# A mixer's seven block products: two weight sums by accumulating DMA, quadrant-wise weights, another product order

## The reference

```
def mixer_block(u, cos, sin, w_in, conv_w, q_norm_g, k_norm_g, w_conv_out, w_attn_out, w_o):
    proj = u @ w_in
    cb, cc, cx, q, k, v, gc, ga = split_columns(proj)
    z = depthwise_conv_centred(cc * cx, conv_w)
    y_conv = (cb * z) @ w_conv_out
    ...
    y_attn = bidirectional_gqa(q, k, v) @ w_attn_out
    merged = jax.nn.sigmoid(gc) * y_conv + jax.nn.sigmoid(ga) * y_attn
    return merged @ w_o
```

## Time and profile before

| | before |
|---|---|
| time, median of 3 runs | 1936.64 us (1935.13 to 1938.69) |
| profiled execution: span from first to last instruction | 1937.6 us |
| PE busy | 1576.1 us (81% of the span) |
| DVE busy | 683.6 us (35%) |
| ACT / POOL busy | 303.4 us (16%) / 13.0 us (1%) |
| bytes by DMA | 554.48 MB, mean 286 GB/s |
| granted TensorE clock, mean | 0.913 |

### The profile page before, as it was taken

The page is one execution under the profiler, slowest core; times in us unless marked ns, Lnnn a source line. Parts: engine busy times, 40 slices in busy tenths (PEclk is TensorE's granted clock), DMA queues, the critical chain, the costliest instruction groups (busy, mean ns, idle before and its releaser), DMA issues.

```text
span 1937.6 us, 22198 instructions
## 1 busy us (share of the span) xinstructions
PE 1576.1 (81%) x9674; PEld 958.1 (49%) x9674; DVE 683.6 (35%) x1421; ACT 303.4 (16%) x806; POOL 13.0 (1%) x39
## 2 busy tenths in 40 slices
PE   8999999999999999856655756556666557799999
PEld 6675566755599995322212222212222122357886
DVE  2673455734486873311111111101111111244533
ACT  0243313433112102000000000000000000213220
POOL 0000000000000000000000000000000000000000
PEclk9999999999999999988778887788787788899999
DMA  9752277413334466999999999999999999954300
GB/s 378 264 138 71 87 272 239 124 51 135 129 137 174 146 236 270 388 431 431 430 431 432 431 430 430 429 427 426 424 426 431 432 431 431 374 205 165 126 14 22
DMA packets 87787, 554.48 MB, mean 286 GB/s; under 512 B 4512, under 2 KB 11424, under 8 KB 74112
## 3 DMA queue, kind: packets, MB, share of 16 engines
q1 hardware_dynamic: 86544, 548.81, 70.4%
q0 software_dynamic: 1136, 4.10, 0.6%
HBM read 551.85 MB, written 1.05 MB: 285 GB/s over the span
## 4 chain that ended last, share of the span: by engine, by line
PE 59%; DMA 35%; DVE 4%; ACT 1%; issue 1%; SPq 0%; POOL 0%; DVEq 0%; ACTq 0%; POOLq 0%
PE bank L677 26%; DMA ring<-in_w 22%; DMA arena<-in_w 12%; PE bank L1154 8%; PE bank L704 6%; PE bank L686 6%; PE bank L1182 3%; PE bank L665 3%; PE bank L1467 1%; PE bank L875 1%; PE bank L809 1%; PE bank L789 1%; DMA prm<-in_pk 1%; DVE arena L2122 0%; DVE arena L2402 0%
## 5 line engine op out<-in xcount | busy, mean ns | idle before, releaser
L1154 PE MATMUL bank<-ring,arena 128*32 128x512 f32 x1216 | 289.1, 732 | 152.0 <-DMA arena<-in_w 100.7
L677 PE MATMUL bank<-arena,ring 128*128 128x128 f32 (+1 forms) x2528 | 393.7, 315 | 0.5 <-DVE arena L3071 0.5
L677 PEld LDWEIGHTS bank<-arena,ring 128*128 128x128 f32 x2528 | 357.2, 191 | 28.2 <-issue 4.5
L1154 PE MATMUL bank<-arena 128*32 128x512 f32 x832 | 234.1, 734 | 100.2 <-DMA ring<-in_w 100.2
L1154 PEld LDWEIGHTS bank<-ring,arena 128*32 128x32 f32 x1216 | 72.1, 131 | 274.6 <-issue 274.6
L677 PE MATMUL bank<-ring,arena 128*128 128x512 f32 (+3 forms) x520 | 205.2, 544 | 1.7 <-ACT tmp L1523 0.8
L1154 PEld LDWEIGHTS bank<-arena 128*32 128x32 f32 x832 | 56.7, 131 | 187.3 <-issue 187.1
L1182 PE MATMUL bank<-ring,arena 128*32 128x512 f32 x576 | 119.3, 660 | 25.2 <-DMA arena<-in_w 13.9
L677 PEld LDWEIGHTS bank<-ring,arena 128*128 128x128 f32 x520 | 96.1, 190 | 84.0 <-issue 72.3
L704 PE MATMUL bank<-ring,arena 128*128 128x512 f32 (+1 forms) x320 | 129.1, 561 | 4.6 <-DVE arena L2003 2.2
L686 PE MATMUL bank<-arena,ring 128*64 128x256 f32 x1024 | 112.7, 380 | 0.0
(11 more groups left out here) (395 smaller groups left out, 1482.7 us busy)
## 6 DMA issues: line engine op xcount, KB each, us to landing
ring<-in_w SPq DMA_DIRECT2D x53, 4096.0 KB, 31.7
arena<-in_w SPq DMA_DIRECT2D x35, 4096.0 KB, 36.9
ring<-in_w_in SPq DMA_DIRECT2D x40, 2048.0 KB, 8.2
ring<-in_w_mod SPq DMA_DIRECT2D x6, 2048.0 KB, 11.9
ring<-in_w_out SPq DMA_DIRECT2D x6, 2048.0 KB, 7.9
arena<-in_w SPq DMA_DIRECT2D x6, 2048.0 KB, 10.7
ring<-in_w SPq DMA_DIRECT2D x6, 2048.0 KB, 11.7
ring<-in_w_out SPq DMA_DIRECT2D x16, 512.0 KB, 9.1
```

Source lines behind the costliest of these rows:

```text
L677: i = te.matmul(ps, lhsT, rhs, start=n0 + k == 0, stop=n0 + k == n - 1)
L1154: m = te.matmul(ps[32 * j:32 * j + 32, :], LM.xg[:, f, 128 * k + 32 * j:128 * k + 32 * j + 32], vs[j][:, 512 * (k % 2):512 * (k % 2) + 512 ...
```

## The change

Four things. First, the seven weights come to the chip a second time as `w_seven`, laid out by quadrant: `w_seven[k, q]` is quadrant q of projection k, 128 rows of 8 KB; `load` now reads two quadrants at once. Second, T1 and T3 are no longer made by DVE. For T1, SP loads one quadrant straight into T1's place (`first_sum`, 1 MB) and POOL issues a DMA that adds another quadrant to it in SBUF; for T3, POOL issues one that adds a quadrant to the weights in `w1[:, 0:4]`. T2 and T4 stay on DVE. Since such a DMA only adds, the signs of sums and results change along. Third, PE's order in a projection is P1, P2, P5, P6, P3, P4, P7 where it was P1 to P7, and DVE's steps follow. Fourth, SP now waits, for each T1 load, until P4 of the projection before is done, ahead of the next projection's weights; and `wo2` is issued ahead of units 0 and 1.

```diff
+            def first_sum(k):
+
+                name, old = SEVEN[k], SEVEN[k - 1] if k else None
+                for w in at.all(*([("mm", "P", old, 4), ("T", old, 2)] if k else [("used", ("os", 1, 1))])):
+                    s.wait_ge(*w)
+                le.dma_start(L2.t1.rearrange("p c n -> p (c n)"), w_seven[k, 2]).then_inc(*t1.inc())
+                at.put(("t1", name), t1.sem, t1.n)
             for k, name in enumerate(SEVEN):
                 for g in range(2):
-                    w, o = wide[name][0], wide[name][1] + 512 * g
-                    load((name, g), (whole, w[:, :, o:o + 512]), slot=(2, 0)[k % 2] + g)
+                    load((name, g), (lambda v: v.rearrange("p (q c) n -> p q (c n)", q=2),
+                                     w_seven[k, 2 * g:2 * g + 2].rearrange("q p n -> p q n")), slot=(2, 0)[k % 2] + g)
+                if name != "ya":
+                    first_sum(k)
...
             s.wait_ge(*at.of("mm", "P", "cb", 7))
             s.wait_ge(*at.of("z", 7))
             unit(4, LM.early[2])
+            first_sum(SEVEN.index("ya"))
+            wv = w_o_2[0].rearrange("(c p) n -> p c n", p=128)
+            for g in range(2):
+                load(("wo2", g), (whole, wv[:, :, 512 * g:512 * g + 512]), slot=g)
...
-                ready(("T", name, 2), ("S", {"yc": 1, "ya": 2}.get(name, 0)))
-                times(("P", name, 3), L2.t2, sums[1], (7 * n + 2) % 4)
-                yield
-                times(("P", name, 4), L2.t1, sums[0], (7 * n + 3) % 4)
-                yield
-                ready(("T", name, 3))
-                times(("P", name, 5), w1[:, 0:4, :], sums[2], (7 * n + 4) % 4)
-                yield
-                times(("P", name, 6), w1[:, 4:8, :], sums[3], (7 * n + 5) % 4)
+                ready(("T", name, 3), ("S", {"yc": 1, "ya": 2}.get(name, 0)))
+                times(("P", name, 5), w1[:, 0:4, :], sums[2], (7 * n + 2) % 4)
+                yield
+                times(("P", name, 6), w1[:, 4:8, :], sums[3], (7 * n + 3) % 4)
                 t.also("used", (name, 1))
+                yield
+                ready(("T", name, 2))
+                times(("P", name, 3), L2.t2, sums[1], (7 * n + 4) % 4)
+                yield
+                ready(("T", name, 1))
+                times(("P", name, 4), L2.t1, sums[0], (7 * n + 5) % 4)
...
-                if k == 1:
-                    ready(("mm", "P", old, 4) if old else ("used", ("os", 1, 1)))
-                    ve.tensor_tensor(L2.t1, w1[:, 0:4, :], w0[:, 0:4, :], ALU.subtract).then_inc(*v.done("T", name, 1))
                 if k == 2:
                     ready(("T", name, 1), ("mm", "P", old, 3) if old else ("used", ("os", 1, 1)))
-                    ve.tensor_tensor(L2.t2, w1[:, 4:8, :], L2.t1, ALU.subtract).then_inc(*v.done("T", name, 2))
-                if k == 3:
-                    ready(("T", name, 1))
-                    ve.tensor_tensor(w1[:, 0:4, :], w1[:, 4:8, :], w1[:, 0:4, :], ALU.subtract).then_inc(*v.done("T", name, 3))
+                    ve.tensor_tensor(L2.t2, w1[:, 4:8, :], L2.t1, ALU.add).then_inc(*v.done("T", name, 2))
+                    v.also("used", (name, 1), "sums")
...
-                    if n:
-                        weight_sum(name, 4)
-                    yield
-                    to_sum(L2.s2, name, 3, L2.s1, ("ev", "P", name, 1))
+                    yield
                     if name == "cb":
                         tap(4)
-                    part_sum(name, 11, 2, L2.s1)
+                    ready(("ev", "P", name, 1))
+                    part_sum(name, 11, 2, L2.s1, L2.y1)
+                    yield
+                    weight_sum(name, 2)
+                    weight_sum(name, 4)
+                    yield
+                    to_sum(L2.s2, name, 3, L2.s1)
+                    to_sum(L2.s3, name, 5, L2.s2)
                     yield
                     to_sum(L2.y1, name, 4, L2.s2)
-                    if new:
-                        weight_sum(new, 1)
-                    yield
-                    to_sum(L2.s3, name, 5, L2.s2)
                     part_sum(name, 22, 4, L2.s3, L2.s2)
-                    yield
                     part_sum(name, 12, 6, L2.y1)
...
+            t1_sums, t3_sums = Slot(t1_sum_sem), [Slot(e) for e in t3_sum_sem]
+            for k, name in enumerate(SEVEN):
+                ready(("w", (name, 1)))
+                ge.dma_start(weights((name, 1))[:, 0:4, :].rearrange("p c n -> p (c n)"), w_seven[k, 3], accum_op=ALU.add
+                             ).then_inc(*t3_sums[k % 2].inc())
+                at.put(("T", name, 3), t3_sums[k % 2].sem, t3_sums[k % 2].n)
+                ready(("t1", name))
+                ge.dma_start(L2.t1.rearrange("p c n -> p (c n)"), w_seven[k, 0], accum_op=ALU.add).then_inc(*t1_sums.inc())
+                at.put(("T", name, 1), t1_sums.sem, t1_sums.n)
```

More of the change, by code:

```diff
@@ L220, in program @@
             qn_rope_a_3, kn_nope_a_3, kn_rope_a_3, qn_b_3, kn_b_3, w_branch_a_3, w_branch_b_3, w_out_3,
-            rope_cs, w_mod, w_vd, w2_last, pk1, pk2, pk_router, pk3, pos3, bgate3, out):
+            rope_cs, w_mod, w_vd, w2_last, w_seven, pk1, pk2, pk_router, pk3, pos3, bgate3, out):
     ctx = ExitStack()
@@ L237, in program @@
         ada_c_sem = sem("ada_c_loaded")
+        t1_sem, t1_sum_sem = sem("t1_loaded"), sem("t1_summed")
+        t3_sum_sem = [sem(f"t3_summed{k}") for k in range(2)]
         h_sem = [sem(f"h{tt}_loaded") for tt in range(2)]
@@ L461, in load @@
                 for w in at.all(*([("used", users[i])] if users[i] else []),
-                                *([("used", users[i], "sums")] if users[i] and users[i][0] in SEVEN and users[i][1] == 0
-                                  else [])):
+                                *([("used", users[i], "sums")] if users[i] and users[i][0] in SEVEN else [])):
                     s.wait_ge(*w)
@@ L577, in sync_program @@
                 unit(u, LM.early[u])
-            wv = w_o_2[0].rearrange("(c p) n -> p c n", p=128)
-            for g in range(2):
-                load(("wo2", g), (whole, wv[:, :, 512 * g:512 * g + 512]), slot=g)
             s.wait_ge(*at.of("sum", "yc", 21))
@@ L1684, in mixer_branches @@
                     old = SEVEN[n - 1] if n else None
-                    ready(("mm", "P", name, 1), *([("sum", old, 11)] if old else []))
+                    ready(("mm", "P", name, 1), *([("ev", "P", old, 3)] if old else []))
                     se.copy(L2.s1, heads(bank("P", name, 1)[:, :], 128)).then_inc(*a.done("ev", "P", name, 1))
@@ L2382, in token_sums @@
                 behind()
-                ve.tensor_tensor(s4, xT[:, 4:8, lo], s2, ALU.subtract).then_inc(*v.done("S", n))
+                ve.tensor_tensor(s4, xT[:, 4:8, lo], s2, ALU.add).then_inc(*v.done("S", n))
             def mixer_branches():
@@ L2414, in part_sum @@
                     behind()
+                    op = ALU.subtract if part in (12, 22) else ALU.add
                     if name in work:
                         both = other if to_be is None else to_be
-                        ve.tensor_tensor(both, ps, other, ALU.add).then_inc(*v.done("ev", "P", name, k))
+                        ve.tensor_tensor(both, ps, other, op).then_inc(*v.done("ev", "P", name, k))
                         behind()
@@ L2429, in part_sum @@
                     else:
-                        ve.tensor_tensor(to, ps, other, ALU.add).then_inc(*v.done("ev", "P", name, k))
+                        ve.tensor_tensor(to, ps, other, op).then_inc(*v.done("ev", "P", name, k))
                         v.also("sum", name, part)
@@ L2435, in to_sum @@
                     behind()
-                    ve.tensor_tensor(dst, heads(bank("P", name, k)[:, :], 128), other, ALU.add
+                    ps = heads(bank("P", name, k)[:, :], 128)
+                    ve.tensor_tensor(dst, *((other, ps) if k == 4 else (ps, other)), ALU.subtract if k == 4 else ALU.add
                                      ).then_inc(*(v.step() if k == 4 else v.done("ev", "P", name, k)))
@@ L2472, in mixer_branches @@
                         token_sums(2, L2.oT, L2.late_sums)
-                    if new:
-                        weight_sum(new, 3)
                     yield
@@ L3315, in _last_by_columns, with _by_quadrant @@
     return i["w2_2"][0, 60:64].reshape(4, 128, 4, 4, 256).transpose(3, 1, 0, 2, 4).reshape(4, 128, 4096)
+def _by_quadrant(i):
+    import numpy as np
+    w = [i["w_in_2"][0][:, o:o + 1024] for o in (1024, 4608, 5632, 2048, 0)]
+    w = np.stack(w + [i["w_conv_out_2"][0], i["w_attn_out_2"][0]])
+    return w.reshape(7, 2, 4, 128, 2, 512).transpose(0, 4, 1, 3, 2, 5).reshape(7, 4, 128, 2048)
 def _pack2(i):
@@ L3349 @@
     pk3, pos3, bgate3 = _pack3(inputs, inv3)
-    given = [(n, _by_partition(inputs[n]) if n in ("w1_2", "w3_2", "w2_2") else inputs[n]) for n in _INS] + [("rope_cs", cs), ("w_mod", _modulation_rows(inputs)), ("w_vd", _v_dt(inputs)), ("w2_last", _last_by_columns(inputs)),
```

(1 more changed line is left out.)

14 lines of the change are left out of this document (4 added, 10 removed).

## The result

| | before | after |
|---|---|---|
| time, median of 4 runs | 1936.01 us (1935.13 to 1938.69) | 1950.59 us (1949.87 to 1952.46) |
| ratio after to before | | 1.0075, interval 1.0063 to 1.0086 |
| profiled execution, its own time | 1938.69 us | 1949.87 us |
| its span | 1937.6 us | 1948.1 us |
| first product of cc | 533.47 us | 531.92 us |

The kernel became slower by 14.6 us (12.2 to 16.6 by the interval). The forecast of +6.5 us had the direction and the places of the waits. It had less than half of the size.

A forecast was written before the change was run, and what follows sets the result against it. The prediction took PE to bound the mixer and DMA the experts. Its terms, 0 in cb, +1.5 us at the end of ya and 2 x 2.5 for T1, gave +6.5 us, 1943.1 us, with 8 in 10 between 1934.5 and 1960.

The forecast's parts named there:

- What bounds the kernel: PE bounds the mixer, DMA the experts behind it; PE's loss or gain in the mixer moves the whole rest.
- Part 1: DVE's work: 14 of 28 weight sums go, 32 us, worth at most part of PE's 4.1 us of waits.
- part 2: T2 made late: PE waits 3.2 us in cb, waits of 1.7 and 1.6 go; net -0.1, taken as nothing.
- Part 3: End of ya: PE waits 2.3 us before `wo2` where it waited 0.8, +1.5 us.
- Part 4: T1 by two DMAs: an addition takes 12.8 us, PE waits 2.5 us each in gc and ya, elsewhere hidden.
- Part 5: Queues: SP's wait for P4 ahead of the next weights is hidden, and `wo2` lands 30 us ahead of its use.
- The sum: Whole kernel: 0 (cb) + 1.5 (end) + 2 x 2.5 (T1) = +6.5 us.
- Its base: Profiled span of 1937.6 becomes 1944.1; it lay 1.0 above the median of 1936.6, which gives 1943.1.
- the likeliest case: T1's additions cost a doubled transfer, 11 to 14 us; 1939.5 to 1947 us, chance 0.33.
- dear additions: Rival: additions at 16.8 us, DMA engines as the bound, +21.0 us, 1957.6; chance 0.23.
- Plain-cost additions: Rival: additions take 7.6 to 9.6 us, only the end of ya counts, +1.5 us, 1938.1; chance 0.32.
- The faster one: Rival: freed DVE never holds PE, T2 of cb comes in time, all 4.1 us go, 1932.5; chance 0.12.

The follow-up runs named there:

- cb_taps: Changed kernel with DVE's part 11 and T2 ahead of the last two taps in cb, and part 12 ahead of 22; 1947.49 us, ratio 1.0055.
- ya_end: Changed kernel with DVE's last parts of ya in the order 12, 21, 22, and SP's expert loads behind part 22; 1948.87 us, ratio 1.0067.
- fill_wait: Changed kernel with PE repeating four, three and two quarters of P6 ahead of the waits of gc, cb and ya; 1944.08 us, ratio 1.0046.
- t1_plain: Changed kernel with POOL's T1 transfer copying its quadrant instead of adding it; one run, 1937.5 us.
- spread: Changed kernel with SP holding half of the next weights, and `wo2` at ya, until T1's addition has landed; 1940.73 us, ratio 1.0021.
- hybrid: Products' order and DVE's steps of the kernel before, only T3 by POOL's adding DMA, quadrant-wise weights kept; 1932.96 us, ratio 0.999.

## Why the prediction was right and wrong

- **What bounds the kernel: right.** The loss in the mixer passed through. The experts' stretch took 1158.0 us, and 1155.9 to 1158.2 in the eight kernels of the experiments; the 1159.5 of before is the longest of all, in an execution (1938.69) that lay 2.7 us above its own median.
- **Part 1 and part 2: right.** DVE's 14 sums are gone, PE waits 3.26 us in cb (3.2 forecast) and the waits of 1.7 and 1.6 us are gone. cb_taps removes that wait with an order of DVE's steps alone.
- **Part 3: right.** 2.41 us at the end, 2.3 forecast. ya_end brings back 0.8.
- **Part 4: right mechanism, T1's addition undersized.** I took 12.8 us for an addition "since behind T1's load SP's queue holds 4.2 MB, 10 us, and not a backlog without end". Beside those 4.2 MB it measured 12.3 to 15.1 us, median 13.7, and without them 7.9 to 8.4. So the price was 1.2 us too low in gc (14.0, wait 3.72 against 2.5), and in cx, which I took as hidden, 13.3 us left a wait of 0.51. In ya it was 12.3 and 2.25. The dearest one, 15.1 in cb, landed at 665.1, 3.0 us ahead of DVE's turn for T2. The load ahead took 5.0 us as forecast (6.0 in cb). My estimate for T3 with the same 12.8 us was too high by 5 us, which cost nothing, since T3 was hidden either way. One price for both was the mistake: a single price can't stand for the same transfer with and without company.
- **Part 5: right.** PE waits for no weights, and T1's loads and the next weights land in time. A 2.1 MB load with nothing beside it took 7.8 us in rows of 8 KB, where it took 7.6 in rows of 2 KB, so the longer rows did not make it faster.
- **The sum: a term is missing.** It counts a wait of PE at its own length. Three of the five waits were followed by a stretch at half clock, 4.9 us in all, more than half of what the prediction missed in this stretch of 13.5 us (7.0; the waits' sizes are 1.6). fill_wait shows that the term exists, and is not part of the waits. The waits of before are 1.7 us and shorter, and its rows at 1.00 hold no warning; that longer ones might be priced otherwise was not considered.
- **Its base: right.** To take 1.0 from the span of 1944.1 is to add 6.5 to the median, so 1943.1 does not hang on which execution was profiled. The profiled executions differ by 11.2 us and the medians by 14.6, since the one of before lay 2.7 above its median and that of after 0.7 below. The stretch of the change, 13.5 us, is nearer to the medians' difference.
- **The range and the direction.** 1950.59 lies outside the 1939.5 to 1947 that the likeliest case alone reaches. It is inside the range since that was drawn over the dear additions of 16.8 us, of which none occurred; the clock that filled the gap stands in no case. A slower kernel had a chance of 0.52. So the direction and the places were earned, and that the time fell into the range was in good part luck.
- **The rivals.** Plain-cost additions came true in t1_plain alone, by taking the addition out: 2.6 us above before, where +1.5 was forecast. The dear case had the right sign for T1 and the wrong one for T3: additions differ by what runs beside them. The faster one fell at cb, where DVE reached T2 at 668.14 us. To cost nothing it had to start by 664.9, one weight sum ahead of PE's turn at 667.2, and T1, which it needs, had itself landed only at 665.1.

## What to carry to other kernels

Before work is moved from an engine with slack to a DMA, find what will be in the queues beside it: the same 1 MB addition took 8 us alone and 14 beside 4.2 MB of loads, and an order of loads won most of the loss back. Price a wait of TensorE of over 2 us at its length and, in the upper bound, 1.6 us more for the clock behind it (2.8 once). And freeing an engine that has slack gives little by itself, 0.1% in hybrid; the order in which it makes things decides, as cb_taps shows.

## What the runs showed of the hardware that was not expected

**The clock fell behind some waits and not behind others.** Over all the profiles here PE had 17 waits of 2.25 to 3.72 us in the mixer. With 11 of them the granted clock fell from 1.00 to 0.50, and 1.5 to 1.7 us were lost (2.8 once). It fell at most 1.5 us after PE had resumed, in ya of the changed kernel right as it resumed, and twice while it still stood still, 1.0 us ahead in ya_end's gc and 0.2 ahead in spread's cb. With 6 it did not fall, one of 3.37 us among them. Behind waits of 1.7 us and less it never fell. The same place did both: cb's wait of 3.26 us was followed by a slow stretch in the changed kernel and in spread, and by none in ya_end. The Trainium skill (TensorE: Matmul & The Clock Gate, "What's actually happening") says that the default state is throttled and that activity releases the throttle, and that what watches the activity is free-running and does not start anew with a kernel. The traces agree with the two levels, and a watch that runs by itself would explain why the same wait is at times punished and at times not; no run here tests it, and what decides stays open.

**An adding DMA's price depends on what runs beside it.** In the changed kernel 1 MB by POOL's queue with the addition took 7.9 to 8.4 us alone. Beside SP's 4.2 MB it took 12.3 to 15.1 us, and a plain transfer in the same places 8.4 to 10.2. With 2.1 MB beside it, in spread, the addition took 10.1 to 11.8.
